# Recurrence of a hybrid streaming encoder: where the gate products stand between the small matmuls of the chunked recurrence

## The reference, cut to what matters

```python
def wkv_scan(r, decay, k, v, kk, a, state0):
    def step(S, inp):
        r_t, w_t, k_t, v_t, kk_t, a_t = inp
        sa = jnp.einsum('bhij,bhj->bhi', S, -kk_t)
        S = (S * w_t[:, :, None, :] + sa[..., None] * (kk_t * a_t)[:, :, None, :]
             + v_t[..., None] * k_t[:, :, None, :])
        y = jnp.einsum('bhij,bhj->bhi', S, r_t)
        return S, y
...
def rwkv_branch(cur, prev, state0, g, mix, w0, w_up, a0, a_up, k_k, k_a, r_k, gn_g, gn_b):
    xs = cur + (prev - cur) * mix
    r, k, v, wd, ad = jnp.split(xs, ...)
    decay = jnp.exp(-jnp.exp(-jax.nn.softplus(-(w0 + jnp.tanh(wd) @ w_up)) - 0.5))
    a = jax.nn.sigmoid(a0 + ad @ a_up)
    kk = heads(k * k_k); kk = kk * lax.rsqrt(jnp.maximum(jnp.sum(kk * kk, -1, keepdims=True), 1e-24))
    k = k * (1.0 + (a - 1.0) * k_a)
    y, S = wkv_scan(r, decay, k, v, kk, a, state0)
    ...  # group norm of y, plus sum(r * k * r_k) * v
    return y * jax.nn.silu(g), S
```

## Time and profile before

| | |
|---|---|
| time, median of 3 runs | 1806.29 us (1805.58 to 1806.95) |
| the profiled execution, its own time | 1801.65 us |
| its span, first to last instruction | 1799.9 us |
| TensorE busy over the span | 1707.6 us, 95% |
| VectorE / ScalarE / GpSimd busy | 822.9 / 801.2 / 412.9 us |
| mean granted TensorE clock | 0.976 of 2.4 GHz |

### The profile page before, as it was taken

The page is one execution under the profiler, slowest core; times in us unless marked ns, Lnnn a source line. Parts: engine busy times, 40 slices in busy tenths (PEclk is TensorE's granted clock), DMA queues, the critical chain, the costliest instruction groups (busy, mean ns, idle before and its releaser), DMA issues. The chain is left out here.

```text
span 1799.9 us, 48546 instructions
## 1 busy us (share of the span) xinstructions
PE 1707.6 (95%) x21338; PEld 1399.9 (78%) x21338; DVE 822.9 (46%) x1196; ACT 801.2 (45%) x1657; POOL 412.9 (23%) x283
## 2 busy tenths in 40 slices
PE   6899999999997999999789999999999998969999
PEld 5688888888886888999667777777777776647787
DVE  4244445444444411222346565555655556624332
ACT  5465666666654422223434444444444443324320
POOL 3322212222110000000213444334443342310000
PEclk9899999999998999999889999999999998979999
DMA  5312111112134322214211212212121123356652
GB/s 213 109 68 76 52 60 70 44 63 89 44 108 165 137 80 85 84 63 145 88 64 51 70 51 74 57 51 70 51 74 57 51 80 130 109 208 233 212 167 92
DMA packets 119137, 170.87 MB, mean 95 GB/s; under 512 B 39568, under 2 KB 78992, under 8 KB 118672
## 3 DMA queue, kind: packets, MB, share of 16 engines
q1 hardware_dynamic: 109568, 153.29, 25.9%
q10 hardware_dynamic: 9360, 14.49, 2.2%
HBM read 113.21 MB, written 55.06 MB: 93 GB/s over the span
## 5 line engine op out<-in xcount | busy, mean ns | idle before, releaser
L620 PE MATMUL a_ps_proj<-a_w_hi,a_x_hi 128*128 128x512 f32 x384 | 156.8, 408 | 7.4 <-ACT a_qk L403 7.4
L620 PE MATMUL a_ps_proj<-a_w_hi,a_x_lo 128*128 128x512 f32 x384 | 150.9, 393 | 0.0
L620 PE MATMUL a_ps_proj<-a_w_lo,a_x_hi 128*128 128x512 f32 x384 | 150.4, 392 | 0.0
L1020 DVE SCALAR_TENSOR_TENSOR j_out<-j_ps,j_rest,j_part 128x512 f32<-128x512 f32 (+2 forms) x65 | 41.9, 644 | 219.0 <-ACT j_last_cols L966 172.5
L543 DVE SCALAR_TENSOR_TENSOR a_stage<-a_ps_s,a_new_bias 128x256 f32<-128x256 f32 x64 | 27.2, 425 | 242.5 <-PE a_ps_s L647 242.5
L2133 PE MATMUL r_ps_gate<-gate_w_hi,gate_x_hi 128*128 128x512 f32 x272 | 116.7, 429 | 7.8 <-POOL r_kiclr_rest L1479 6.0
L2133 PE MATMUL r_ps_gate<-gate_w_lo,gate_x_hi 128*128 128x512 f32 x272 | 116.2, 427 | 0.0
L2133 PE MATMUL r_ps_gate<-gate_w_hi,gate_x_lo 128*128 128x512 f32 x272 | 115.8, 426 | 0.0
L964 ACT ACTIVATE j_part<-j_last_cols,j_shift_in 128x1 f32<-128x1 f32 x65 | 19.2, 295 | 211.7 <-PE j_ps L1045 211.7
L1791 DVE TENSOR_TENSOR r_w_mat<-r_ps_w,consts 128x512 f32<-128x512 f32 x83 | 57.3, 691 | 106.9 <-PE r_ps_w L2017 106.9
L2447 PE MATMUL o_ps_y<-out_w_hi,o_z_hi 128*128 128x512 f32 x240 | 98.0, 408 | 2.5 <-DVE o_z_lo L2370 2.5
(11 more groups left out here) (340 smaller groups left out, 4481.0 us busy)
## 6 DMA issues: line engine op xcount, KB each, us to landing
a_xT<-in_x_T SPq DMA_DIRECT2D x17, 512.0 KB, 3.4
scratch_xT<-a_xT SPq DMA_DIRECT2D x17, 512.0 KB, 2.7
raw<-scratch_xT SPq DMA_DIRECT2D x17, 512.0 KB, 4.1
scratch_gates<-r_gate_out SPq DMA_DIRECT2D x34, 256.0 KB, 2.4
z_gate<-scratch_gates SPq DMA_DIRECT2D x17, 512.0 KB, 3.9
xs<-scratch_xs_T SPq DMA_DIRECT2D x15, 576.0 KB, 4.5
a_x<-in_x_prompt SPq DMA_DIRECT2D x16, 512.0 KB, 6.3
scratch_xs_T<-j_out ACTq DMA_DIRECT2D x39, 192.0 KB, 1.9
```

The costliest lines, as they stand in the source:

```text
L620: mm = nc.tensor.matmul(ps_proj[:], a[n % 2][:, k, :], w[:, k, g * AW:(g + 1) * AW], start=(k == 0 and i == 0), stop=(k == KT - 1 and i == 2))
L1020: last = nc.vector.scalar_tensor_tensor(out=out[j][:, 0:n], in0=ps[j][:, 0:n], scalar=rest[:, c:c + 1], in1=part[j][:, 0:n], op0=ALU.mult, ...
```

## The change

The gate products of a tile come in seven blocks (six of 6 and one of 12) instead of twelve of 4. Four of the sixes stand in the long pauses of levels 0 to 3; the short pauses hold plain float32 jobs: kk_sum, turn of v, bonus, decay/iclr, turn of b and k. For this, kk_sum and the turn of v move from the body before into `front`, the bank order changes with them, and the rounded halves of the gate input (`x_hi`, `x_lo`) get a second buffer, so that they can be made a body ahead. The recurrent inputs `xs` come in one transfer instead of two and later in the body; the load of the sample states moves from the start of the phase to body 15, since the second buffer takes its place. Gram pair 0 now stands ahead of state product 0, and Gram pair 1 ahead of from_state 1. The new order of TensorE by keys: W0, kk_sum, Q0, 6, W1, turn of v, Q1, 6, W2, bonus, Q2, 6, W3, decay/iclr, Q3, 6, W4, turn of b and k, Q4, from_state 0, solve 0, Gram pair 0, state product 0, read_out 0, Gram pair 1, from_state 1, 6, solve 1, 6, state product 1, read_out 1, 12.

```diff
-        (w_hi, w_lo), (x_hi, x_lo), x_raw = shared.gate_w, shared.gate_x, shared.raw
+        (w_hi, w_lo), x_raw = shared.gate_w, shared.raw
+        x_hi, x_lo = ([even, at(n, [P, KT, P], AT_GATE_X + (2 + i) * D, F32R)] for i, (even, n) in enumerate(zip(shared.gate_x, ("x_hi1", "x_lo1"))))
...
-        JOB_ORDER = ((("bonus", -1), ("decay", 0), ("k_tok", -1), ("B0", -1), ("B1", -1), ("v_tok", 0)),
-                     (("iclr", 0), ("b_tok", -1), ("K0", -1), ("K1", -1), ("kk_sum", 0), ("v_swap", 0)))
+        JOB_ORDER = ((("v_tok", -1), ("bonus", -1), ("decay", 0), ("k_tok", -1), ("B0", -1), ("B1", -1)),
+                     (("kk_sum", -1), ("v_swap", -1), ("iclr", 0), ("b_tok", -1), ("K0", -1), ("K1", -1)))
...
-        LEVEL_AT, CHAIN_AT = 4.1, (20.5, 26.85)
-        GRAM_AT = (25.05, 28.15)
+        LEVEL_AT["p"], CHAIN_AT["p"], SOLVE_AT["p"], READ_AT["p"], U_AT["p"] = 4.8, (22.5, 27.9), (23.6, 30.5), (26.1, 33.5), (24.3, 31.2)
+        LEVEL_AT["s"], CHAIN_AT["s"], SOLVE_AT["s"], READ_AT["s"], U_AT["s"] = 4.1, (20.5, 26.85), (22.9, 29.25), (26.2, 32.4), (23.7, 30)
+        GRAM_AT, GATE_AT = (24.4, 26.8), ((3.3, 6), (8.1, 6), (12.9, 6), (17.7, 6), (28.9, 6), (31.3, 6), (34.2, 12))
```

```diff
+            load_gate_x(2)
-            sp.dma_start(states[:], io["state_in"]).then_inc(states_loaded, 16)
...
+                    sp.wait_ge(gate_written, 2 * DEC)
+                    sp.dma_start(states[:], io["state_in"]).then_inc(states_loaded, 16)
...
-                    yield (13.2, 33.5)[j]
+                    yield (20.3, 37.4)[j]
...
+            def front(t, u, mode):
+                yield 15
+                if t + 2 <= DEC:
+                    need(sp, t, "rkr", "rhat")
+                    for name in ("iclr", "v_tok", "v_swap"):
+                        was_written(sp, t + 1, name)
+                    load_xs(t + 2, u)
```

```diff
-                for j in range(2):
-                    yield (12.4, 32.5)[j]
-                    copy_gates(t, j)
+                yield 19.4
+                copy_gates(t, 0)
                 if t < DEC:
-                    yield 32.6
+                    yield 24.8
                     split_x(t + 1)
+                yield 37.2
+                copy_gates(t, 1)
```

```diff
-                yield 32.45
+                yield 2.4
                 ps, read = written(dve, t, "kk_sum")
...
-                    yield GRAM_AT[n] + 1.2
+                    yield {"B0": 26.2, "K0": 26.3, "B1": 28, "K1": 28.1}[name]
                     ps, read = written(dve, t, name)
...
-                        yield (25.3, 31.7)[n]
+                        yield (26.05, 33.4)[n]
                         dve.wait_ge(s_written, 2 * t + n + 1)
```

```diff
-                yield 31.4
+            def front(t, u, mode):
+                yield 1.1
                 need(pe, t, "kk_sq")
                 ps, done = free_bank(t, "kk_sum")
...
-                yield 35.3
+                yield 5.9
                 turn_two(t, "v_tok", xs[u][:, 8:12], "v_swap", xs[u][:, 8:12])
-            def front(t, u, mode):
-                yield 11.5
+                yield 10.7
                 need(pe, t, "rkr")
                 ps, done = free_bank(t, "bonus")
...
-                yield 21.8
+                yield 20.3
                 need(pe, t, "kt", "bt")
...
             def gates(t, u, mode):
-
-                for j, keys in enumerate(((1.1, 3.2, 5.2, 7.3, 9.3, 11.4), (13.4, 17.5, 19.6, 23.6, 28.9, 30))):
-                    for b, key in enumerate(keys):
-                        yield key
-                        gate_products(t, j, b)
+                done = 0
+                for key, count in GATE_AT:
+                    yield key
+                    gate_products(t, done, count)
+                    done += count
```

More of the change, by code:

```diff
@@ L1428, in out @@
                     load_x_half(1, j)
-            def mix(t, u, mode):
-                if t < 2:
-                    return
-                yield 0.1
-                was_written(sp, t - 1, "v_tok")
-                past(sp, t - 1, "rkr")
-                load_xs(t, u, slice(4, CT), xs_loaded)
-                yield 20
-                past(sp, t - 1, "rhat")
-                load_xs(t, u, slice(0, 4), r_loaded)
+            def front(t, u, mode):
[5 more added lines that the diff above has]
+                    load_xs(t + 2, u)
             def tail(t, u, mode):
@@ L1460, in back @@
                                      states[:, :, now, :].rearrange("p c b d -> p c (b d)")).then_inc(stored, 16)
-            tiles(sp, nothing, back, mix, tail, gates, first_gates, out)
+            tiles(sp, front, back, tail=tail, gates=gates, first_gates=first_gates, out=out)
             for j in range(2):
@@ L1724, in mix @@
                 last.then_inc(ready["fac"], 1)
-                yield 32.45
-                ps, read = written(dve, t, "kk_sum")
-                past(dve, t, "ahat", "bmul")
-                nc.vector.tensor_scalar(kk_n[:], ps[:], 1e-24, None, ALU.max).then_inc(read, 1)
             def scaled(u, kind, x, shifted, mode):
@@ L1746, in front @@
                     nc.vector.memset(runs(g_run, mode)[:, :, :, 0], 1.0).then_inc(dec_copied, 1)
+                yield 2.4
+                ps, read = written(dve, t, "kk_sum")
+                past(dve, t, "ahat", "bmul")
+                nc.vector.tensor_scalar(kk_n[:], ps[:], 1e-24, None, ALU.max).then_inc(read, 1)
                 yield 6.3
@@ L1810, in back @@
                 else:
-                    yield LEVEL_AT * 3
+                    yield LEVEL_AT[mode] * 3
                     need(dve, t, "ahat", "rhat")
@@ L1837, in tail @@
             def tail(t, u, mode):
-                yield 2
+                yield 3.2
                 need(dve, t, "ps_y")
@@ L1995, in back @@
                 for l in range(L):
-                    yield LEVEL_AT * l
+                    yield LEVEL_AT[mode] * l
                     if l == 0:
@@ L2087, in back @@
                 for n in range(NCH):
-                    at = CHAIN_AT[n]
+                    at = CHAIN_AT[mode][n]
                     yield at
@@ L2101, in back @@
                         to_streams(0)
-                    yield at + 2.4
+                    yield SOLVE_AT[mode][n]
                     pe.wait_ge(rhs_ready, 2 * t + n + 1)
@@ L2107, in back @@
                     solve(n)
-                    yield (24.5, 30.9)[n]
+                    yield (25.5, 32.9)[n] if mode == "p" else (24.5, 30.9)[n]
                     pe.wait_ge(u_ready, 2 * t + n + 1)
@@ L2115, in back @@
                         last.then_inc(s_written, 1)
-                    yield (26.2, 32.4)[n]
+                    yield READ_AT[mode][n]
                     last = read_out(n)
@@ L2121, in back, with gate_products @@
                     to_streams(1)
-            def gate_products(t, j, b):
-                for i in range(4 * b, 4 * b + 4):
+            def gate_products(t, first, count):
+                for n in range(first, first + count):
+                    j, i = divmod(n, 3 * KT)
                     k, m = divmod(i, 3)
```

95 lines of the change are left out of this document (47 added, 48 removed).

## The result

The changed kernel takes 1884.38 us (median of 4 runs, 1884.11 to 1884.61), the kernel before 1806.62 beside it: the ratio is 1.0422, 95% interval 1.0402 to 1.0442. The forecast was 1817.5, range 1800 to 1825. It had the sign right, and for the most part the place (the bodies of the prompt tiles), and the size wrong by 67 us.

A forecast was written before the change was run, and what follows sets the result against it. TensorE's order and gaps were taken to set the prompt bodies' time; 15 x 0.67 - 2.3 + 3.6 + 0.5 = 11.9 us, carried over to 1806.29, gave a forecast of 1817.5 us, range 1800 to 1825.

The forecast's parts named there:

- The prices: TensorE pieces: time from a piece's first start to the next one's, such as 1.59 us for a block of six.
- The walk: One prompt body followed along TensorE's new order, adding piece times and waits counted from step ends: next W0 at 37.77 us.
- the drain: TensorE at each gate block, changing from 64 x 64 to 128 x 128 work and back: 0.34 us beside its products.
- The wait for v_tok: Level 2 of each body: the bonus product waits for ScalarE's v_tok, so Q2 starts 0.40 us behind its limit.
- The term that decides: TensorE stands 2.12 us before Gram pair 1, because VectorE's state update precedes the masks of B0 and K0.
- The main case: Prompt bodies: the wait at Gram pair 1 eats the saved blocks, 1817.5 us, own range 1812 to 1823; chance 0.62.
- Costed at nothing: Second buffer's copy and subtraction on ScalarE and GpSimd, the later whole xs transfer and the moved states load: no added time.
- Rival 4: TensorE's clock falls behind each 2.1 us gap, some 2 us more in each of 16 bodies: 1850; chance 0.05.
- The edges: Outside the repeated bodies: start 2.3 us less, body 15 3.6 us more, body 16 0.5 us more.
- (2): Small waits in the bodies are covered, GpSimd's chain early and the rhs copy free for TensorE: 1806; chance 0.12.
- (3): Masks of B0 and K0 run before VectorE's state update, so TensorE does not stand at Gram pair 1: 1784; chance 0.16.
- (5): VectorE's queue, with kk_n and y_sum behind the first mask, delays a level by another 0.5: 1825; chance 0.05.

The follow-up runs named there:

- experiment 1: The changed kernel with VectorE's masks of B0 and K0 put ahead of the state update of chunk 0: 1825.36 us, ratio 1.0113.
- experiment 2: The changed kernel with GpSimd's x_lo moved behind its addition to the masked Gram products, out of the state update's time: 1835.89 us, ratio 1.0165.
- experiment 3: The kernel before with only the Gram pairs moved, pair 0 ahead of state product 0 and pair 1 ahead of from_state 1: 1829.11 us, ratio 1.0126.
- experiment 4: The changed kernel with the first block of six after the wait moved between read_out 0 and Gram pair 1: 1841.68 us, ratio 1.0199.

## Why the prediction was wrong

**The prices were right.** The walk up to W4 came out within 0.07 us, the block of six at 1.60 for 1.59, the drain at 0.33 for 0.34. **The wait for v_tok** was given 0.40 and measured 0.43, released 10.25 us into the body for 10.23.

**The term that decides had the right mechanism.** Experiments 1 to 3 show it. Its size by itself is 2.00 in the walk's measure (1.80 as the profile counts a wait), for 2.12. The main case, "the wait at Gram pair 1 eats the saved blocks", would have been about right if it had stood alone: the kernel of experiment 2 has it and took 1835.9, of which some 10 are the key of body 16, and some the clock of a few bodies and the pauses in issue.

**The step that failed is "Costed at nothing".** It said that "the second buffer moves the same copy and subtraction on ScalarE and GpSimd, both under half busy". A busy share says nothing about what runs beside an instruction. GpSimd's x_lo moved from the end of the body into the state update and made the multiply up to 1.9 us longer, 1.4 in the mean, and that lies inside the very wait that decides. From state product 0 to Gram pair 1 it is 4.46 us in the mean, where experiment 3 has 2.92 and the walk 3.04: 1.42 us a body over the walk. Moving x_lo away gives back 46 of the 78 us (experiment 2), since most of the slow clock goes with it.

**Rival 4, the clock, had 0.05 and the right price.** It gave "some 2 us more in each of 16 bodies" for Gram pair 1 and from_state 1; 1.43 were measured for these two, 1.88 with the block of six behind them. The chance was too low for a reason that the text had in hand: it had seen the clock low behind a gap of 2.75 us, had seen no gap that left it up, and forecast one of 2.12. The runs have both outcomes at such lengths: behind 1.8 us the clock fell in 3 of 13 bodies of experiment 2 and in 1 of 16 of experiment 3, behind 2.06 to 2.09 us in 5 of 7 of experiment 4, and in the changed kernel, from 2.08 us up, in all 15. What else decides is open; in the changed kernel the waits of 2.08 to 2.31 us all stand behind a pause in issue of 1.12 to 1.24 us. In the sum below the clock is the largest term; with its chance of 0.05 it was left out of the range.

**The pauses in issue were not in the walk:** 0.76 us a body, of which 0.61 stand ahead of state product 0; the others lie in the stretch from there to Gram pair 1 and are in its 4.46. The kernel before has four of them, which a walk over one body doesn't show.

| us a body | |
|---|---|
| walked, next W0 | 37.77 |
| state product 0 to Gram pair 1 (4.46 for 3.04) | 1.42 |
| Gram pair 1, from_state 1 and a block at the lower clock | 1.88 |
| pauses in issue ahead of state product 0 | 0.61 |
| sum | 41.68 |
| measured, mean of 15 | 42.10 |

The 0.42 left lie ahead of state product 0. Of these 0.18 stand in every body: body 14, which has no pause, reaches state product 0 at 25.12, where the walk had 24.94. The rest I leave open; the bodies of the kernel before vary by as much, with a mean of 37.61 for the 37.23 of the one body that I took for all.

**The edges.** Body 16 was given 0.5, by the store of the gates and what is queued behind it; 13.3 were lost, 10 of them by a key of ScalarE that the walk of the prompt tiles did not reach. Body 15 was given 3.6 and lost 6.9. It lost them elsewhere than the other bodies: its wait at Gram pair 1 is only 1.32 us, but TensorE waits for v_tok 1.25 us, not 0.40, the granted clock behind that is 0.55 (1555.78 to 1559.60), and two pauses in issue take 0.65 us together. The start brought 4.9 for 2.3.

**The other rivals.** (2), the small waits covered, is out: they stood. (3), the masks through ahead of the update, did not happen, and experiment 1 shows that two keys would have brought it about, and what it is worth. (5) did not show in the levels.

The Trainium skill, "SBUF — State Buffer", section "SBUF: two separate sides", says that GpSimd and a VectorE operation with two SBUF inputs share a port pair that one of them holds for its whole instruction. By that rule the state add, which reads PSUM, is free and the multiply, which reads SBUF twice, blocks. The trace agrees with it: 0.42 beside x_lo for the add at 1106.09, 2.24 for the multiply. I had not weighed it.

## What to carry to other kernels

When a change moves work on an idle engine, ask what will run beside it, and whether that is inside a wait that decides: the share of busy time does not answer this. A hand-written key has to be followed in every mode and every phase that shares the engine, not only in the body that repeats; the last body may hold another phase's pieces at close keys. And a gap on TensorE costs more than its length once the clock falls behind it; where the trace has no gap of that length that left the clock up, the forecast needs a range that holds both cases.

## What the runs showed of the hardware

- TensorE's pauses in issue lie 126.3 matmuls with their loads apart, or multiples of that, in every kernel here: one packet of the instruction queue (16.4 KB, 252.5 instructions) holds as many. Each of 219 pauses over 0.2 us, up to 2.45, ends 1.18 to 1.72 us after the packet with the next instructions has landed. They show in stretches of small float32 matmuls (0.029 us each); a block of six 512-column products ahead of the chain removed nearly all. What makes one packet set out later than another no run shows.
- VectorE's multiply of two SBUF operands went from 0.42 to 2.24 us beside a GpSimd subtraction of 2.34 us, and ended 0.28 us after it. An addition with a PSUM operand stayed at 0.42.
- The granted clock fell behind gaps of 2.08 to 3.63 us in 15 of 15 bodies of the changed kernel, behind gaps of 2.06 to 2.09 us in 5 of 7 (experiment 4) and of 1.8 us in 4 of 29 (experiments 2 and 3). The work behind it, to solve 1, took 5.42 us in the mean for 3.54 in the changed kernel.
